# A delta mixer with the convolution's taps moved out of the triangular solver and one projection cut in four

## The reference, cut to what matters

```python
proj = x @ w_in        # split into dq, dk, dv, dz, da, dbeta, glu, c_q, c_kv, k_r, gate_logits
y_dn = deltanet_branch(dq, dk, dv, dz, da, dbeta, ...)
y_cv = conv_branch(glu, ...)
y_mla = mla_branch(c_q, c_kv, k_r, cos, sin, ...)
merged = gates[0] * y_dn + gates[1] * y_cv + gates[2] * y_mla
```

```python
sol = lax.linalg.triangular_solve(a_mat, rhs, left_side=True, lower=True, unit_diagonal=True)
u, w = sol[..., :dv], sol[..., dv:]
v_new = u_i - w_i @ state
o = q_dec_i @ state + qk_i @ v_new
state = state * exp(gl_i) + k_dec_i^T @ v_new
```

```python
h = u[..., :512] * jax.nn.sigmoid(u[..., 512:])
h = causal_depthwise_conv(h, dw_w) + dw_b
```

## Time and profile before

| | us |
|---|---|
| median of 3 runs | 2447.11 (2447.03 to 2456.01) |
| the profiled execution | 2446.66 |
| its span, first to last instruction | 2444.9 |
| TensorE busy in the span | 2352.5 (96%) |
| VectorE busy | 1625.3 (66%) |
| ScalarE busy | 1084.7 (44%) |
| POOL busy | 311.0 (13%) |

### The profile page before, as it was taken

The page is one execution under the profiler, slowest core; times in us unless marked ns, Lnnn a source line. Parts: engine busy times, 40 slices in busy tenths (PEclk is TensorE's granted clock), DMA queues, the critical chain, the costliest instruction groups (busy, mean ns, idle before and its releaser), DMA issues.

```text
span 2444.9 us, 32236 instructions
## 1 busy us (share of the span) xinstructions
PE 2352.5 (96%) x13225; PEld 2004.6 (82%) x13225; DVE 1625.3 (66%) x1799; ACT 1084.7 (44%) x1258; POOL 311.0 (13%) x419
## 2 busy tenths in 40 slices
PE   5999999999999999999999899999999998999998
PEld 4777868888878888888799789788788898888887
DVE  6898558778876755554676776655644757858544
ACT  3344554444435544344465335444344454244442
POOL 3110201101103000100004600000100007300000
PEclk9999989999999999999999899999999999999999
DMA  9996429868975566465553235556456442434653
GB/s 336 357 323 227 138 96 318 297 218 310 326 249 174 186 232 209 159 206 185 194 161 113 90 104 173 173 189 224 157 189 219 143 128 77 140 121 155 207 186 124
DMA packets 330460, 477.61 MB, mean 195 GB/s; under 512 B 19835, under 2 KB 267994, under 8 KB 330314
## 3 DMA queue, kind: packets, MB, share of 16 engines
q1 hardware_dynamic: 307514, 396.33, 49.3%
q0 software_dynamic: 22800, 79.23, 8.9%
HBM read 474.45 MB, written 1.05 MB: 194 GB/s over the span
## 4 chain that ended last, share of the span: by engine, by line
PE 79%; DVE 9%; issue 3%; DMA 3%; ACT 3%; DVEq 3%; POOL 1%; SPq 0%; POOLq 0%; ACTq 0%
PE ps L940 23%; PE ps L942 23%; PE ps L941 23%; DVE w_lo L2267 3%; DMA raw<-in_ffn_wu_dram 2%; ACT w_hi L1789 1%; PE ps L1015 1%; DVE diag L2872 1%; DVE mix_mem L2387 1%; PE ps L1563 1%; DVE parts L2356 1%; POOL n_rstd L744 1%; DVEq L2403 1%; DVEq L2874 1%; PE ps L1556 0%
## 5 line engine op out<-in xcount | busy, mean ns | idle before, releaser
L2267 DVE TENSOR_TENSOR w_lo<-raw,w_hi 128x2048 fp32r<-128x2048 f32 (+2 forms) x374 | 823.7, 2204 | 392.0 <-ACT w_hi L1789 386.4
L1789 ACT ACTIVATE w_hi<-raw 128x2048 fp32r<-128x2048 f32 (+1 forms) x370 | 687.5, 1858 | 465.1 <-PE ps L942 178.8
L940 PE MATMUL ps<-w_hi,x_hi 128*128 128x512 f32 x1504 | 599.1, 398 | 12.1 <-DVE x_lo L2290 6.8
L942 PE MATMUL ps<-w_hi,x_lo 128*128 128x512 f32 x1504 | 588.9, 392 | 0.0
L941 PE MATMUL ps<-w_lo,x_hi 128*128 128x512 f32 x1504 | 587.3, 390 | 0.0
L940 PEld LDWEIGHTS ps<-w_hi,x_hi 128*128 128x128 f32 x1504 | 283.7, 189 | 72.1 <-issue 8.7
L942 PEld LDWEIGHTS ps<-w_hi,x_lo 128*128 128x128 f32 x1504 | 283.2, 188 | 61.1
L941 PEld LDWEIGHTS ps<-w_lo,x_hi 128*128 128x128 f32 x1504 | 284.0, 189 | 56.7 <-issue 0.5
L940 PE MATMUL ps<-x_hi,w_hi 128*128 128x256 f32 (+1 forms) x992 | 286.9, 289 | 0.0
L941 PE MATMUL ps<-x_lo,w_hi 128*128 128x256 f32 (+1 forms) x992 | 282.2, 284 | 0.0
L942 PE MATMUL ps<-x_hi,w_lo 128*128 128x256 f32 (+1 forms) x992 | 282.1, 284 | 0.0
(11 more groups left out here) (415 smaller groups left out, 2844.4 us busy)
## 6 DMA issues: line engine op xcount, KB each, us to landing
raw<-in_w_in_dram SPq DMA_DIRECT2D x96, 512.0 KB, 4.7
raw<-in_ffn_wg_dram SPq DMA_DIRECT2D x88, 512.0 KB, 4.6
raw<-in_ffn_wu_dram SPq DMA_DIRECT2D x88, 512.0 KB, 5.8
raw<-in_ffn_w_gate_dram SPq DMA_DIRECT2D x88, 512.0 KB, 4.0
raw<-in_ffn_w_up_dram SPq DMA_DIRECT2D x88, 512.0 KB, 5.0
raw<-in_ffn_wd_dram SPq DMA_DIRECT2D x80, 512.0 KB, 5.3
raw<-in_ffn_w_down_dram SPq DMA_DIRECT2D x80, 512.0 KB, 4.3
spare<-in_w_ada_dram POOLq DMA_DIRECT2D x40, 512.0 KB, 5.7
```

What stands on the lines that cost most here:

```text
L940: pe.matmul(dst, wh, vh, start=start, stop=False, skip_group_check=True)
L942: return pe.matmul(dst, wl, vh, start=False, stop=stop_, skip_group_check=True)
L1789: return f(w_hi[at.hi_slot()][:, cols], raw[at.raw_slot()][:, cols], ACT.Copy)
L2267: return v.tensor_tensor(w_lo[s][:, cols], raw[s][:, cols], w_hi[at.hi_slot()][:, cols].bitcast(F32), ALU.subtract)
```

## The change

Five things are done in `mix_b`, in both layers.

- VectorE keeps a count of taps for each of its tiles. Tiles 0 and 1 get four rounds before the wait for `g_mm`, three after `dec_in`; then one round of all three tiles is done before the wait for `kk_mm`. The solver's steps have no taps.
- VectorE makes the low part of chunk n0 + 19 behind `level(1)` in place of chunks n0 + 19 and n0 + 20 ahead of `level(0)`; chunk n0 + 20 comes behind the solver, n0 + 21 behind `v_new`. The four taps before the state's copy become one. The last call runs until tile 2 has its 31 rounds: 16 rounds, of which 9 have all three tiles.
- ScalarE rounds no halves of a chunk in steps 1 and 2.
- TensorE makes projection 19 in four pieces of 12 matmul records, behind `hd_stats`, `s_mm`, `ws_mm` and `o_mm`, and projection 20 in its two column halves, one before and one behind the sums of squares.
- SP loads `uq` after `s_mm` and `ukv` after `o_mm`, with a semaphore for each.

```diff
+                sp.wait_ge(s_mm, l + 1)
+                sp.dma_start(uq[:, :, :], a["mla_w_uq_2"][l:l + 1].rearrange("o (k p) n -> p (o k) n", p=P))\
+                    .then_inc(mla_uq, 16)
                 sp.wait_ge(o_mm, l + 1)
...
                 sp.dma_start(ukv[:, :, :], a["mla_w_ukv_2"][l:l + 1].rearrange("o (k p) n -> p (o k) n", p=P))\
-                    .then_inc(mla_w, 16)
+                    .then_inc(mla_ukv, 16)
...
+                def proj_part(s, g, m, ks):
+
+                    h = w_hi[s[0]][:].rearrange("p (k n) -> p k n", k=KT)
+                    lw = w_lo[s[1]][:].rearrange("p (k n) -> p k n", k=KT)
+                    for k in ks:
+                        last = split_mm(ps[:, proj_bank(g), T * m:T * m + T], h[:, k, m * P:m * P + P],
+                                        lw[:, k, m * P:m * P + P], x_hi[:, k, :], x_lo[:, k, :], k == 0, k == KT - 1)
+                    return last
...
                 last.then_inc(hd_stats, 1)
+                pe.wait_ge(evac, evac0 + 17)
+                s19 = take()
+                proj_part(s19, 19, 0, range(4))
                 pe.wait_ge(u_copied, l + 1)
...
                 last.then_inc(s_mm, 1)
+                proj_part(s19, 19, 0, range(4, KT))
                 pe.wait_ge(s_ready, l + 1)
...
                 last.then_inc(ws_mm, 1)
+                proj_part(s19, 19, 1, range(4))
                 pe.wait_ge(v_new, l + 1)
...
                 last.then_inc(o_mm, 1)
+                used(proj_part(s19, 19, 1, range(4, KT)))
                 head_rows(4, 3, hd_rstd, call_h(l, 1) + 1)
-                proj(19)
+                proj(20, ms=(0,))
                 pe.wait_ge(hd_scaled, l + 3)
                 head_sums(4, work, 3, hd_sq, sq_at(l, 1))
-                proj(20)
+                cols_chunk(proj_bank(20), x_hi, x_lo, ms=(1,))
                 head_rows(8, 4, hd_rstd, call_h(l, 2) + 1)
...
-                    if s == 1:
-                        ahead(n0 + 20)
-                        first_half()
-                    elif s == 2:
-                        second_half()
+                ahead(n0 + 21)
                 act.wait_ge(u_mm, l + 1)
...
                 ahead(n0 + 16)
+                dve.drain()
+                taps(4, (0, 1))
                 dve.wait_ge(g_mm, l + 1)
...
                 v.tensor_scalar(emat[:], emat[:], 0.0, None, ALU.min).then_inc(dec_in, 1)
+                taps(3, (0, 1))
                 ahead(n0 + 17)
...
                 ahead(n0 + 18)
                 dve.drain()
+                taps(1)
                 dve.wait_ge(kk_mm, l + 1)
...
                 v.tensor_tensor(amat[:], amat[:], tmat[:], ALU.mult).then_inc(a_ready, 1)
-                ahead(n0 + 20)
                 dve.drain()
                 level(0)
...
                 level(1).then_inc(b_ready, 1)
+                ahead(n0 + 19)
                 dve.wait_ge(tok_mm, l + 1)
...
                         level(s + 1).then_inc(b_ready, 1)
                         d_out(l * HALVES + (2 * s + 1))
-                    taps(1)
-                    if s == 3:
-                        ahead(n0 + 21)
+                ahead(n0 + 20)
+                taps(1)
                 dve.wait_ge(hd_stats, call_h(l, 1) + 1)
...
-                taps(4)
+                taps(1)
                 dve.wait_ge(s_mm, l + 1)
...
                     .then_inc(v_new, 1)
+                ahead(n0 + 21)
                 taps(2)
...
-                taps(TAPS - tap_at[0])
+                taps(TAPS - tap_at[2])
                 dve.drain().then_inc(cv_dve, 1)
```

More of the change, by code:

```diff
@@ L378, in block_kernel @@
         cv_dve = sem("cv_dve")
-        mla_w = sem("mla_w")
+        mla_uq = sem("mla_uq")
+        mla_ukv = sem("mla_ukv")
         mla_mm = sem("mla_mm")
@@ L682, in _ @@
                 branch("dn_w_o_2")
+                sp.wait_ge(s_mm, l + 1)
+                sp.dma_start(uq[:, :, :], a["mla_w_uq_2"][l:l + 1].rearrange("o (k p) n -> p (o k) n", p=P))\
+                    .then_inc(mla_uq, 16)
                 sp.wait_ge(o_mm, l + 1)
-                sp.dma_start(uq[:, :, :], a["mla_w_uq_2"][l:l + 1].rearrange("o (k p) n -> p (o k) n", p=P))\
-                    .then_inc(mla_w, 16)
                 sp.dma_start(ukv[:, :, :], a["mla_w_ukv_2"][l:l + 1].rearrange("o (k p) n -> p (o k) n", p=P))\
-                    .then_inc(mla_w, 16)
+                    .then_inc(mla_ukv, 16)
                 gates(1)
@@ L1440, in mix_b, with proj @@
                 evac0 = call_e(l, 0)
-                def proj(g, n=256):
+                def proj(g, n=256, ms=None):
                     if g >= 3:
                         pe.wait_ge(evac, evac0 + (g - 2))
-                    cols_chunk(proj_bank(g), x_hi, x_lo, n=n)
+                    cols_chunk(proj_bank(g), x_hi, x_lo, n=n, ms=ms)
+                def proj_part(s, g, m, ks):
[5 more added lines that the diff above has]
+                    return last
                 c = border_b(l, 0)
@@ L1640, in mix_b @@
                 last.then_inc(o_mm, 1)
+                used(proj_part(s19, 19, 1, range(4, KT)))
                 head_rows(4, 3, hd_rstd, call_h(l, 1) + 1)
-                proj(19)
+                proj(20, ms=(0,))
                 pe.wait_ge(hd_scaled, l + 3)
                 head_sums(4, work, 3, hd_sq, sq_at(l, 1))
-                proj(20)
+                cols_chunk(proj_bank(20), x_hi, x_lo, ms=(1,))
                 head_rows(8, 4, hd_rstd, call_h(l, 2) + 1)
-                pe.wait_ge(mla_w, l * 32 + 32)
+                pe.wait_ge(mla_uq, l * 16 + 16)
                 for h in range(HEADS):
@@ L1673, in mix_b @@
                                   low[:, k, :], start=(k == 0), stop=(k == 2))
+                pe.wait_ge(mla_ukv, l * 16 + 16)
                 for h in range(HEADS):
@@ L2858, in log_decay, with taps @@
                         .then_inc(g_ready, 1)
[L2860 to L2866, removed]
+                tap_at = [0, 0, 0]
+                def taps(n, tiles=(0, 1, 2)):
+                    for _ in range(n):
+                        for t in tiles:
+                            sh = tap_at[t]
+                            if sh == TAPS:
+                                continue
+                            tap_at[t] += 1
+                            j = TAPS - 1 - sh
                             wcol = cols3[:, 4 * j + t:4 * j + t + 1]
@@ L2874, in taps @@
                         dve.drain()
-                    tap_at[0] += n
                 def level(s):
@@ L2964, in mix_b @@
                 last.then_inc(tok_done, 1)
-                ahead(n0 + 19)
                 def d_out(value):
```

## The result

The changed kernel takes 2432.36 us (median of 8 runs, 2422.08 to 2436.68) beside 2447.82 of the kernel before on the same chip (8 runs, 2441.79 to 2456.01): ratio 0.9936, interval 0.9916 to 0.9956, so 15.5 us faster, 0.64%. The forecast was 2425.7, within 2418 to 2434: the side is right, and 15.5 came of the 20.9 us that the sum gave. The profiled execution took 2433.86.

What follows compares the result with a forecast made beforehand. TensorE, busy 96% of the span, was taken to bound the kernel, losing time to waits and half clock. Gains 2 x 4.6 + 6.5 + 7.8 = 23.5, less 2.6 for the clock, gave 20.9: 2425.7 us, range 2418 to 2434.

Steps and rivals of the forecast that it cites:

- the half cases of two rivals: POOL late by half would give 2431 us; half of the solver's gain would give 2430.4.
- The solver: Removing waits for ScalarE's and VectorE's copies in the solver's steps starts L1610 4.6 us earlier per layer.
- Behind the solver: L1610 to L1150 falls to 27.3 us before clock costs, a gain of 6.5 in layer 0 and 7.8 in layer 1.
- the late root: Before L1150: VectorE's moment is out at 23.4 us, POOL's root follows, and TensorE stands still for 3.7.
- The clock: Half clock costs 0.8 us at L1610 and 0.5 behind the root's wait per layer, 2.6 in all.
- The full price: Half clock in full at L1610 and behind the root's wait, both layers: 5.2 us, time 2428.4.
- The root's 3.65: POOL's root ahead of L1150 takes 3.65 us and starts 0.2 after the moment.
- POOL was not late: Rival: POOL's adds, slowed by VectorE, delay the root before L1150; 2438.4 us, chance 0.10.
- The solver was not as long as before: Rival: another wait replaces those removed in the solver, leaving only the gain behind it; 2435.0 us, chance 0.08.
- nothing was lost at the end: Rival: last taps and chunk 24 come out uncovered, 13.2 us go back; 2439 us, chance 0.06.
- the clock never stayed low throughout: Rival: small matmuls and pieces hold TensorE at 1.2 GHz from L1610 to L1150; 2463 us, slower, chance 0.04.
- Costs taken as nothing: Taps ahead of the solver, chunk 19's low part there, moved loads and rounding, and the later rotation were costed at nothing.

Runs made afterwards that it cites:

- run 3: Changed kernel with chunk 23's two half roundings back on ScalarE in solver steps 1 and 2: solver's first record to L1621 19.15 and 19.07 us, 17.96 before.
- run 5: Changed kernel with VectorE's taps and chunk 20's low part back in the solver's steps: solver's first record to L1621 20.99 and 19.65 us, 17.96 before.
- run 9: run 8 with taps of two tile rows in solver steps 1 to 3 and two tap groups moved behind the branch's merge: 2414.79 us, ratio 0.9869.
- run 10: The changed kernel measured again without any edit: 2432.99 us (6 runs), ratio 0.9929 to the kernel before.
- Run 7: Changed kernel with three taps issued before chunk 23's low part behind the heads' moment: root 1.83 us in both layers, squares to L1152 7.20 and 7.73.
- run 2: Changed kernel with VectorE's moment of the heads issued ahead of two groups of taps: L1621 to L1152 28.02 and 25.25 us, 30.84 and 30.92 before.
- run 6: Changed kernel with the twenty one-column records dealt out in piece 1 of projection 19: 5.97 us to L1647, L1152 only 0.2 and 0.1 earlier.
- run 1: Changed kernel with projections 19 and 20 whole again in their old places: L1621 to L1152 30.01 and 31.04 us, 30.84 and 30.92 before.
- run 8: Changed kernel with idle products, dealt-out one-column records, more taps ahead of the first statistics, earlier moment and second root, taps before chunk 23's low part: 2426.01 us, ratio 0.99.

## Why the prediction was right, and where its size was off

The measured 2432.36 us lie in the stated range, but beyond 2429.4, the worst end that the forecast's own costs gave. The range reached to 2434 to take in the half cases of two rivals, and neither rival came true; that the result lies inside is in part luck.

- **The solver**, forecast 4.6 a layer: 22.6 and 22.9 became 17.96, 4.6 and 5.0. Right. Runs 3 and 5 show 1.1 to 1.2 of it for the roundings and 1.7 for the low part; the rest, for the taps in front of the low part and the half clock behind the wait, is argued.
- **Behind the solver**, forecast 27.3 and 0.8 for the clock: 30.84 and 30.92 in the profiled execution. TensorE's own chain was right, 23.6 in the forecast and 23.52 in run 9; the late root was named, with VectorE's moment ending last (2.62 us of waiting where 3.7 was forecast). The moment came 27.1 behind L1621 instead of 23.4 (the forecast's terms add up to 23.2; the moment's own 0.17 us is the rest). In layer 1 of run 10, at full clock, it came at 24.3: most of its delay is that of the slow records ahead of it, and the other 0.9 is VectorE's taps, two groups of six at 3.65 and 3.43 us where the forecast had 3.1 and 2.5.
- **The clock is the term that was sized wrong.** The prediction took 0.8 of 1.6 at L1610 ("one of two"), nothing behind the statistics, and 0.5 behind the root: 2.6 for both layers. In the profiled execution L1621 took 1.6 longer in each layer, piece 1 and the state 1.5 (7.5 against 6.0 from the statistics to L1647); 2.8 of these 3.1 reached L1152, going by the 28.09 of run 10. From L1152 to L1689 1.4 and 1.0 came on top of the 24.66 forecast. That makes 8.0, 5.4 more than forecast. With 0.8 a layer for the taps, and less the 0.7 that the solver and its start gave beyond the forecast, it is the 6.3 between 20.9 and the 14.6 of the marks. Half for L1621 was a fair mean (9 of 16 ends); the stretch behind the one-column records was the one overlooked. The full price by the section "HAM oscillation" of the Trainium skill's "TensorE: Matmul & The Clock Gate", 5.2, came nearer but also lacked this place: TensorE was busy for 3.05 of 3.05 us just ahead of that fall, with no gap.
- **The root's 3.65** was read off as its length. Run 7 shows that about half of it was a wait for the low part issued in front of it, in the kernel before as well.
- **The rivals.** POOL was not late in the changed kernel (it waited 2.68 for the moment), but in part because the moment was late too: from its first root's end to its last tap it took 16.3 us where 14.3 was forecast, and at full clock it waited only 0.98 (run 10). It became late once the moment came early (run 2) or its own first root came late (run 6). The solver was not as long as before, nothing was lost at the end (from L1689 to the statistics 26.2 us in both kernels), and the clock never stayed low throughout.
- **Costs taken as nothing** held: with the taps ahead of the solver VectorE still waits 1.90 and 0.98 us there (the earlier trace rows had 5.60 and 3.66), the first product follows the projection without a wait, and step 2 of the solver starts 9.23 us behind it (9.29 and 9.45 before).
- **The pieces** were given no line of their own in the sum, only their place in the chain; run 1 shows that in this order they bring nothing.

## What to carry to other kernels

When a wait is taken away, follow the other engine's queue to the next thing that it hands over: here filling TensorE's waits paid nothing while VectorE's moment was issued behind work that could wait. (Run 9 has both mended, so it does not show what the pieces are worth by themselves then.) Look at what each engine issues in the moment that a short instruction on POOL is due, for here the low part of 2.28 us, a two-operand instruction of VectorE started first, made a root of 1.7 to 1.8 us last 3.65. And judge an edit of a few microseconds by marks inside the stage, over several executions, since the granted clock alone moves them by 1.6 at a time.

## What was not expected of the hardware

The granted clock fell to half behind stretches in which TensorE was busy all the time, but mostly with records of one column (3.05 of 3.05 us busy, then 0.56 in layer 0). It did so in 10 of 14 layers, and no longer in that place when these were dealt out between records of a projection (5.97 against 7.53 us, 0 of 6). With seven idle products of 256 columns around the solver's end L1621 ran at full clock in both layers of runs 8 and 9, for 0.2 to 0.4 us of delay. A POOL root of 8 columns took 1.67 to 1.83 us, or 3.65 with VectorE's low part started in front of it; VectorE's taps of 0.4 us each beside it did no such harm (1.83).
